# Order of work in the first layer of a two-layer encoder step: latent gates ahead of differential gates, two output tiles begun with four blocks

## The reference

```
layer 0:  h = x @ w_in  ->  q_lat, ckv, krope, g_mla, dq, dk, dv, g_diff
          o_mla  = latent attention (8 heads), o_diff = differential attention (4 heads)
          o_diff = rmsnorm(o_diff, subln_g) * (1 - lam_init)
          o = concat[o_mla * silu(g_mla), o_diff * silu(g_diff)] @ w_out
          x = layernorm(ALPHA * x + o)
layer 1:  q, k, v, g = x @ w_in ;  o = stick-breaking attention (16 heads)
          x = layernorm(ALPHA * x + (o * silu(g)) @ w_out)
```

## Time and profile before

| | us |
|---|---|
| three runs, lowest, median, highest | 892.22, 892.53, 892.58 |
| the profiled execution, its time | 890.0 |
| its span, first to last instruction | 888.2 |
| PE busy in the span | 835.0 (94%) |
| DVE busy, ACT busy, POOL busy | 538.2 (61%), 402.6 (45%), 65.5 (7%) |

### The profile page before, as it was taken

The page is one execution under the profiler, slowest core; times in us unless marked ns, Lnnn a source line. Parts: engine busy times, 40 slices in busy tenths (PEclk is TensorE's granted clock), DMA queues, the critical chain, the costliest instruction groups (busy, mean ns, idle before and its releaser), DMA issues.

```text
span 888.2 us, 17057 instructions
## 1 busy us (share of the span) xinstructions
PE 835.0 (94%) x6676; PEld 710.5 (80%) x6676; DVE 538.2 (61%) x1082; ACT 402.6 (45%) x897; POOL 65.5 (7%) x94
## 2 busy tenths in 40 slices
PE   6999999999999999889999999999999999969885
PEld 5996788887888888577899998888888888757674
DVE  3275356555565676877833466666566776766876
ACT  4233433343444334412225455755575565856610
POOL 2120000000000000011210010000000010000012
PEclk9999999999999999999999999999999999989998
DMA  6631121211413334312132334323423333342122
GB/s 220 151 99 61 48 59 56 61 31 32 138 49 109 122 105 138 128 63 97 54 114 96 117 105 126 97 92 127 131 85 105 121 115 98 97 132 74 62 73 94
DMA packets 67390, 86.25 MB, mean 97 GB/s; under 512 B 6001, under 2 KB 53905, under 8 KB 67313
## 3 DMA queue, kind: packets, MB, share of 16 engines
q1 hardware_dynamic: 63568, 74.47, 26.6%
q0 software_dynamic: 3744, 10.70, 3.8%
HBM read 74.25 MB, written 10.90 MB: 96 GB/s over the span
## 4 chain that ended last, share of the span: by engine, by line
PE 67%; issue 19%; DVE 6%; ACT 4%; POOL 2%; DMA 1%; DVEq 0%; SPq 0%; POOLq 0%; ACTq 0%
PE turn L902 22%; PE value L902 15%; PE pair L902 13%; PE proj L902 9%; PE turn L940 2%; POOL rstd L875 2%; DVE w_lo L1533 1%; PE turn L1117 1%; PE proj L940 1%; PE value L940 1%; PE proj L1117 1%; ACT w_hi L1312 1%; PE pair L940 0%; DMA x_sb<-in_x_prompt_dram 0%; PE value L1117 0%
## 5 line engine op out<-in xcount | busy, mean ns | idle before, releaser
L1533 DVE TENSOR_TENSOR w_lo<-stage,w_hi 128x512 fp32r<-128x512 f32 (+1 forms) x144 | 97.1, 682 | 100.4 <-ACT w_hi L1312 100.1
L902 PE MATMUL turn<-w_hi,xT_hi 128*128 128x256 f32 (+2 forms) x356 | 113.2, 318 | 12.6 <-DVE w_lo L1533 8.8
L902 PE MATMUL turn<-w_hi,xT_lo 128*128 128x256 f32 (+2 forms) x356 | 109.4, 307 | 0.0
L902 PE MATMUL turn<-w_lo,xT_hi 128*128 128x256 f32 (+2 forms) x356 | 109.2, 307 | 0.0
L1312 ACT CAST w_hi<-stage 128x512 fp32r<-128x512 f32 (+1 forms) x144 | 87.4, 614 | 31.8 <-PE turn L902 9.7
L902 PE MATMUL value<-w_hi,xT_hi 128*128 128x256 f32 (+2 forms) x252 | 82.2, 326 | 4.0 <-DVE w_lo L1533 2.4
L902 PEld LDWEIGHTS turn<-w_hi,xT_hi 128*128 128x128 f32 x356 | 68.0, 191 | 18.3 <-DVE xT_lo L1538 8.1
L902 PE MATMUL value<-w_lo,xT_hi 128*128 128x256 f32 (+2 forms) x252 | 78.9, 313 | 0.0
L902 PE MATMUL value<-w_hi,xT_lo 128*128 128x256 f32 (+2 forms) x252 | 78.8, 313 | 0.0
L1392 ACT ACTIVATE work<-pair,peak 128x512 f32<-128x512 f32 (+4 forms) x80 | 41.0, 516 | 66.0 <-DVE peak L1634 63.8
L902 PEld LDWEIGHTS turn<-w_hi,xT_lo 128*128 128x128 f32 x356 | 68.1, 191 | 3.2
(11 more groups left out here) (510 smaller groups left out, 2000.2 us busy)
## 6 DMA issues: line engine op xcount, KB each, us to landing
stage<-in_w_in_odd_dram SPq DMA_DIRECT2D x64, 256.0 KB, 2.6
stage<-in_w_in_even_dram SPq DMA_DIRECT2D x44, 256.0 KB, 2.8
k_c<-in_cache_sb_k_dram SPq DMA_DIRECT2D x32, 256.0 KB, 3.2
v_c<-in_cache_sb_v_dram SPq DMA_DIRECT2D x32, 256.0 KB, 2.8
x_sb<-in_x_prompt_dram SPq DMA_DIRECT2D x8, 512.0 KB, 4.7
mlaK<-in_cache_diff_k_dram SPq DMA_DIRECT2D x8, 512.0 KB, 3.9
mlaK<-in_cache_diff_v_dram SPq DMA_DIRECT2D x8, 512.0 KB, 4.3
stage<-in_w_out_even_dram SPq DMA_DIRECT2D x16, 256.0 KB, 2.5
```

The lines of the kernel that those rows point to most:

```text
L902: return nc.tensor.matmul(o, l, r, start=first, stop=last)
L1533: v.tensor_tensor(piece(w_lo[:, sec % 2, words]), piece(stage[:, n % STAGES, :]), piece(w_hi[:, sec % 2, words].bitcast(F32)), ALU.subtrac ...
```

## The change

In the schedule of layer 0:

- The eight `G` products come ahead of the ten `gd` products, in the attention steps 25 to 32 in place of 35 to 42, and their parts alternate between two row blocks.
- The last steps are in another order: `DS` 5, 6 and 7 each stand one place earlier, and the last two steps are `D` (0, 2) and `D` (0, 3).
- `mcvt`, `ogT`, `gate` and the left output products are put one or two steps earlier, and seven left products stand ahead of `od` instead of five.
- A new job `begin` computes blocks 0 to 3 of the right half of tiles 0 and 1 in its own bank; the later `("out", 0, 2, t, 1)` of these tiles adds blocks 4 to 7 in the same bank.
- Behind `od` the two `post` and the two `norm` and `gate` pairs stand together, and the four conversions of section `out001` behind them in one piece.
- The value products of the `D` steps are scaled out of PSUM by ACT and no longer by DVE.
- The sums of `post` for the sample tile have columns of their own in `ss`, so the next `post` needn't wait for POOL.
- The two vectors of the layer norm are loaded after `ogT` of tile 0, which is now the last.

In layer 1, `sig` and `silu` of a gate stand behind the weight conversion that shares their place, not ahead of it.

```diff
-SECTIONS = [name + i for name in ("A", "dv", "dk", "dq", "gd", "G") for i in "01"]
+SECTIONS = [name + i for name in ("A", "dv", "dk", "dq", "G", "gd") for i in "01"]
...
-    steps += [("D", 1, 3), ("D", 0, 0), ("DS", 5), ("D", 0, 1), ("DS", 6), ("D", 0, 2), ("DS", 7), ("D", 0, 3)]
+    steps += [("D", 1, 3), ("DS", 5), ("D", 0, 0), ("DS", 6), ("D", 0, 1), ("DS", 7), ("D", 0, 2), ("D", 0, 3)]
...
+    for kind, half, order, coming in (("dk", 0, tiles, "dk1"), ("dk", 1, tiles, "dq0"), ("dq", 0, queries, "dq1"), ("dq", 1, queries, "G0"),
+                                      ("G", 0, tiles, "G1"), ("G", 1, tiles, "gd0"), ("gd", 0, gates, "gd1"), ("gd", 1, gates, "out000")):
+        if kind == "G":
+            work += beside([[("G", blk, part)] for part in range(2) for blk in (2 * half, 2 * half + 1)], convert(coming))
+        else:
+            work += beside([[(kind, t, half)] for t in order], convert(coming))
...
-    fills[35].append([("gate", 3)])
+    second = convert("out010")
+    fills[39].append([("gate", 3)])
     fills[40].append([("gate", 2)])
-    fills[46].append([("gate", 1)])
-    second = convert("out010")
-    fills[43].append([("mcvt", 0), ("mcvt", 1)])
-    fills[44].append([("mcvt", 2), ("mcvt", 3)])
-    fills[45] += [[("out", 0, 0, 0, 0)], second[:1]]
-    fills[46] += [[("ogT", 3, 1)], [("out", 0, 0, 1, 0)], second[1:2]]
-    fills[47] += [[("ogT", 2, 1)], second[2:3]]
+    fills[42].append([("mcvt", 0), ("mcvt", 1)])
+    fills[43] += [[("mcvt", 2), ("mcvt", 3), ("ogT", 3, 1)], [("out", 0, 0, 0, 0)], second[:1]]
+    fills[44] += [[("ogT", 2, 1)], [("out", 0, 0, 1, 0)], second[1:2]]
+    fills[45] += [[("out", 0, 0, S_TILE, 0)], second[2:3]]
+    fills[46] += [[("gate", 1)], [("out", 0, 0, 3, 0)], second[3:]]
+    fills[47] += [[("ogT", 1, 1)], [("out", 0, 1, 3, 0)]]
...
-    light, last_sample, last = steps[-3:]
-    right = convert("out001")
-    jobs += [("value", light), ("turn", last_sample), ("dsT", STREAMS - 2), ("ogT", 1, 1), ("out", 0, 0, S_TILE, 0)] + second[3:]
-    jobs += [("turn", last), ("value", last_sample), ("out", 0, 0, 3, 0), ("value", last), ("dsT", STREAMS - 1), ("post", 0)]
-    jobs += [("out", 0, 0, 2, 0), ("od",), ("norm", 0), ("gate", 0), ("post", S_TILE), ("out", 0, 1, 3, 0)] + right[:1]
-    jobs += [("ogT", 0, 1), ("norm", S_TILE), ("gate", S_TILE), ("out", 0, 1, 2, 0)] + right[1:2] + [("ogT", S_TILE, 1)]
-    jobs += [("out", 0, 1, 1, 0)] + right[2:3] + [("out", 0, 1, 0, 0)] + right[3:] + [("out", 0, 1, S_TILE, 0)] + convert("out011")
+    last_sample, light, last = steps[-3:]
+    jobs += [("value", last_sample), ("turn", light), ("out", 0, 1, 1, 0), ("dsT", STREAMS - 1), ("turn", last), ("value", light)]
+    jobs += [("out", 0, 0, 2, 0), ("od",), ("value", last), ("post", S_TILE), ("post", 0), ("out", 0, 1, 2, 0)]
+    jobs += [("norm", S_TILE), ("gate", S_TILE), ("norm", 0), ("gate", 0)] + convert("out001") + [("ogT", S_TILE, 1)]
+    jobs += [("out", 0, 1, S_TILE, 0), ("begin", 0, 0), ("ogT", 0, 1), ("out", 0, 1, 0, 0)] + convert("out011") + [("begin", 0, 1)]
...
-        gates = [[("g", g, 0, 0)], [("g", g, 0, 1), ("sig", g, 0)], [("g", g, 1, 0), ("silu", g, 0)], [("g", g, 1, 1), ("sig", g, 1)]]
+        gates = beside([[("g", g, blk, part)] for blk in range(2) for part in range(2)], convert(f"{after_values}{g}"))
+        for bundle, job in zip(gates[1:], (("sig", g, 0), ("silu", g, 0), ("sig", g, 1))):
+            bundle.append(job)
         queries[0].append(("silu", g, 1))
-        return fill + beside(gates, convert(f"{after_values}{g}")) + beside(queries, convert(f"k{g + 1}")) + [[("gblocks", g)]]
+        return fill + gates + beside(queries, convert(f"k{g + 1}")) + [[("gblocks", g)]]
...
-        if ring:
+        begun = where.get(("begin", job[1], job[3])) if job[0] == "out" and job[2] == 2 else None
+        if begun:
+            where[job] = begun
+        elif ring:
...
+                        if job == units["gd1"][1] and k < 4:
+                            m.then_inc(mix_read, 1)
...
+                    begun = 4 if part == 2 and ("begin", layer, t) in where else 0
+                    if not begun:
+                        wait_bank(pe, job)
+                    for k in ks[begun:]:
...
+                elif kind == "begin":
+
+                    _, layer, t = job
+                    wait_bank(pe, job)
+                    for k in range(4):
+                        pe.wait_ge(ocvt_done, ocvt_no[("ocvt" if layer else "mcvt", k)])
+                        wait_quarter(job, f"out{layer}01", k)
+                        product(ps(job)[:, :], x_block(k, tok(t)), w_block(f"out{layer}01", k * 512, 512), k == 0, False)
...
+                elif kind == "value" and job[1][0] == "D":
+                    _, t, h = job[1]
+                    r = nth[job[1]] % 8
+                    wait_filled(act, job)
+                    nc.scalar.mul(od_n[t][:, h * P:(h + 1) * P], ps(job)[:, 0:P], coef[:, r, 0:1]).then_inc(done, 1)
...
-                        wait_drained(dve, ("value", ("D", t, DH - 1)))
+                        for h in range(DH):
+                            wait_drained(dve, ("value", ("D", t, h)))
...
-                    link(v.tensor_reduce(ss[:, 0, 0:DH], s3, AX_X, ALU.add))
-                    v.tensor_scalar(ss[:, 1, 0:DH], ss[:, 0, 0:DH], 1.0 / (2 * HD), EPS, ALU.mult, ALU.add).then_inc(pow_in, 1)
+                    link(v.tensor_reduce(ss[:, 0, sums_of(t)], s3, AX_X, ALU.add))
+                    v.tensor_scalar(ss[:, 1, sums_of(t)], ss[:, 0, sums_of(t)], 1.0 / (2 * HD), EPS, ALU.mult, ALU.add).then_inc(pow_in, 1)
```

27 lines of the change are left out of this document (9 added, 18 removed).

## The result

The changed kernel is slower. Its median is 906.31 us (four runs, 903.21 to 910.11) against 892.56 for the kernel before in the same session (892.22 to 894.01): a ratio of 1.0153, with a 95% interval of 1.011 to 1.0196. A second comparison gave 906.42 (six runs) and 1.0142 (1.0099 to 1.0185). So the loss is about 1.5%, and the intervals leave no doubt of its sign. The forecast was 901.5 with a range up to 905.5. The sign was right, the size was not: + 13.8 in place of + 9.0.

The account below looks back on a forecast made before the run. PE was taken as the bound, busy for 835.0 of 888.2 us. New holes and clock of 19.4 less 10.4 gone gave + 9.0 on the median of 892.53, so 901.5, range 896.5 to 905.5.

Parts of the forecast that it names:

- start of step 43: Attention step 43, layer 0: PE's work up to it only turned round, so it starts at 350.93 in both kernels.
- wait for the splits of `o_mT`: Step 43: the split now feeds the same step's left product, so PE waits about 2.2 us after two blocks.
- `od`: End of layer 0's attention: claimed to start at 388.0, against 385.05 before.
- hole ahead of the samples' transposes: Behind `od`: PE done at 391.4, samples' gate at 396.5, so a hole of 5.1 us replaces the 2.26.
- hole behind them: Behind the samples' transposes: PE idles 6.0 us for `xT_lo`, behind four `w_lo` and the fourth quarter's load.
- hole at the layer norm: Before layer 1's first transposes: only 2.75 us of product is left as cover, so PE waits about 2.3 for `shift`.
- wait for `q0`: Layer 1's first query product: its 1.70 us wait goes because the conversion of `q0` now precedes `sig`.
- lower clock: Behind the two long holes: 1.7 us lost against 1.6 before, so it cancels; ends 1.6 gained or 3.2 more.
- 4.86 of small waits: Between step 43 and `od`: seven small PE waits, most behind evictions now on ACT or moved products, should go.
- more is lost: Rival, 0.10: low clock over two products (3.2 us) and one 1.7 wait in the attention steps with `G`; 906.4.
- Only the first hole opens: Rival, 0.12: samples' split does not wait for the fourth quarter, second hole about 1.6 us; 897.1.
- the tail's holes do not open: Rival, 0.06: DVE and ACT are ahead by `od`, begun tiles cover the rest; faster, 887.1.

Follow-up runs that it names:

- 2: The changed kernel with the samples' transposes put ahead of the four `out001` weight conversions; 903.19 us, ratio 1.0085 to the kernel before.
- experiment 3: The changed kernel without the two `begin` jobs, right halves of tiles 0 and 1 done in one piece; 901.68 us, ratio 1.0083 to the kernel before.
- kernel 8: The kernel before with only the `G` products put ahead of the `gd` products; 892.68 us, ratio 1.0006.
- experiment 6: The kernel before with only the evictions of the `D` steps' value products moved from DVE to ACT; 892.01 us, ratio 0.9992.
- Experiment 5: The changed kernel with 20 unused matmuls of 512 columns in each of PE's two long holes; 903.59 us, ratio 1.0137 to the kernel before.
- 1: The changed kernel run again without any edit, with a second profile; 906.42 us.
- 10: The changed kernel with samples' `norm` and gate before tile 0's `post`, samples' transposes before the `out001` conversions, nothing begun; 895.51 us, ratio 1.0026 to the kernel before.
- 4: The kernel before with only the changed kernel's order of `sig`, `silu` and conversion in layer 1; 893.31 us, ratio 0.9984.
- 7: The kernel before with the `D` steps' evictions on ACT and layer 1's new order of `sig` and `silu`; 890.14 us, ratio 0.9976.
- 9: The kernel before with `D` evictions on ACT, layer 1's new order, and samples' `norm` and gate directly behind their `post`; 887.95 us, ratio 0.9947.
- run 81: Not a label but a count: the kernel before, unaltered, was run 81 times; median 892.46 us, from 889.34 to 901.65.

## Why the prediction was wrong

By its own steps, with the changed kernel's first profile:

| step | predicted | measured |
|---|---|---|
| start of step 43 | as before, 350.93 | 353.35, 2.4 later |
| wait for the splits of `o_mT` | 2.2 | 2.30 |
| wait for the bank that DVE drains late | 0.3 | 0.41 |
| wait for the bank that ACT drains late | 0.25 | none |
| `od` | 388.0 | 391.15, 388.7 without the 2.4 |
| hole ahead of the samples' transposes | 5.1 | 4.97 |
| hole behind them | 6.0 | 5.15 |
| tile 0's transposes to their product | 1.6 | 1.40 |
| wait for the last quarter of `out011` | 1.33 stays | 1.36 |
| hole at the layer norm | 2.3 | 2.38 |
| wait for `q0` | gone | gone |
| lower clock | 1.7 new, 1.6 gone | 9.8 new, 3.4 gone |

The holes came out as worked out: + 8.9 predicted without the clock, + 7.8 measured, none off by more than 0.9. Experiments 2, 3 and 8 show the cause of the second hole, the cause of the one at the layer norm, and that `G` in other steps is free. The most that is off is 0.85 in the second hole. Of this 0.6 is that the prediction counted 0.5 for the transposes at the full clock; they took 1.12 at the low one, inside the wait for the fourth quarter. Most of the rest is that the fourth `w_lo` started 3.0 behind the end of the first (404.60 - 401.57) and not 3.3. The 4.86 of small waits went too, but for 1.66 of it the reason given, an eviction on DVE, was not the one (experiment 6).

**The step that failed** is "Clock. [...] I take 1.7 here too, so this term cancels." It measured + 6.4 and not + 0.1. The prediction priced one hole's clock by one row of the kernel before, and gave a price to the longest pair only. In the profile the new hole of 2.30 at 359.94 (1.6), the two long ones as one stretch (3.1) and the 2.38 of the layer norm (1.7) are each followed by a low stretch, and only the stretch behind the old 2.26 went: + 4.7 in the tail. Experiment 5 shows this for the long pair by filling it, experiment 3 for the last by taking the hole away. The prediction went through the new holes for their length and not once more for their clock. Nor does one row give the price: the same hole has a low stretch in one profile and none in the next. Counted over the twelve profiles (before, changed, and the ten experiments), with a stretch that starts during the idle time or within 2 us behind it:

| idle time of PE | profiles with it | with a low stretch |
|---|---|---|
| 6.65, between 787 and 809 | 12 | 12 |
| behind `od`, long or two in a row (changed, 1, 2, 3, 10) | 5 | 5 |
| 2.44, between 841 and 865 | 12 | 10 |
| 2.38, layer norm (changed, 1, 2, 5) | 4 | 4 |
| 2.30, splits (all orders of the changed kernel) | 6 | 4 |
| 1.92 or 2.26, samples' transposes (before, 4, 6, 7, 8) | 5 | 3 |
| 1.66 (before, 4, 6, 7, 8, 9) | 6 | 3 |
| 1.70, layer 1 (before, 6, 8) | 3 | 0 |

The kernel before happened to have its stretch behind the 2.26 and none behind the 1.66; kernel 8 had it the other way round. So the clock term is a sum over all holes of a price times a chance, and here the one new price was read behind one hole of one profile. The Trainium skill, page "TensorE: Matmul & The Clock Gate", part 1 on the clock gate, says that the number of slow matmuls behind a cold start differs between runs. These profiles agree in kind; that a whole stretch can be missing is more than this statement says.

The other 1.7 stands ahead of the changed work: the stretch at 188 to 194 lies in steps whose order did not change and in which PE was busy for 6.00 of 6.00 us. It is most of the 2.4 by which step 43 is late; the other 0.8 was already there at 151 us. The profiles have one such early stretch (before, 2, 4, 6, 7, 9, 10) or two (changed, 1, 3, 5, 8), near 153, 189, 205 or 236, each at or within 4 us behind one of the short idle times of 0.2 to 0.4 that stand there in every kernel. Whether these set them off, and whether the changed order gets more of them, is not shown. Kernels 2 and 10, with one, start step 43 at 350.89 and 350.90: where the prediction had it.

Of the rivals, "more is lost" named 906.4, nearly the time that came, by 3.2 for the clock over two products and 1.7 for a wait in the steps with `G`. Its first half is right in kind, its second did not happen, and its sum counts double: 3.2 is the price of two products, and 1.7 for one of them is in the 901.5 already, so by its own prices it comes to 904.7. That 906.4 was met is luck. "Only the first hole opens" was excluded for the right reason, and "the tail's holes do not open" was wrong by the mechanism given against it: DVE's chain starts with `od`. The range was too narrow because its clock bound, 3.2, covered one place, and the low time of whole runs was not in it at all: the kernel before, taken from three runs within 0.4 us, spreads over 12 us when it is run 81 times.

## What to carry to other kernels

Count the clock for every new hole of PE, not for the largest: here a hole of 2.3 us cost up to 4 (with 1.6 to 1.7 behind it in four of six profiles, nothing in two), and a pair of 5 us each 3.1 on top. Take the price from several executions, not from one row. When an operation waits for a chain on another engine, look at what of that engine's queue can stand behind the chain rather than in it: one gate moved ahead of one add gave about 2 us, while grouping like work together (two `post`, four conversions) put 7.2 and 6 us in front of what PE wanted. A pair of profiles with equal matmul counts and unequal PE busy time says at once that the clock has changed and not only the waits.
